# Rounding and splitting outputs at the head of a step, and the queries' rotary sums two slots later, in a prompt attention spread over 76 steps

## The reference, cut to what matters

```
q_nope, q_pe = q[..., :QK_NOPE], q[..., QK_NOPE:]
return q_lat, rope(q_pe, pos), rmsnorm(ckv, kv_norm), rope(kpe, pos)
...
s = jnp.where(kpos[None, :] <= qpos_b[:, None], s, -jnp.inf)
p = jax.nn.softmax(s, axis=-1).astype(ckv.dtype)
return jnp.einsum('bqhk,bkc->bqhc', p, ckv)
```

## Time and profile before

| | us |
|---|---|
| median of three runs | 1499.21 (1498.85 to 1500.34) |
| span of the profiled execution | 1494.5 |
| the profiled execution's own time | not listed; the median is 4.71 above its span |
| prompt attention in it, first scores to last split | 82.0 to 252.3 |
| an odd pair with eight pieces (three of them) | 24.9 |
| an even pair with four pieces (pairs 2, 4, 6) | 18.3 |
| pair 7 with its tail | 24.3 |

### The profile page before, as it was taken

How to read it: one execution, slowest core, us unless ns; L and a number is a source line. 1 busy time by engine, 2 the same in 40 slices (tenths; PEclk the granted TensorE clock), 3 DMA queues, 4 the chain that set the end, 5 groups by cost and what they waited for, 6 DMA issues and landing times.

```text
span 1494.5 us, 28951 instructions
## 1 busy us (share of the span) xinstructions
PE 1416.7 (95%) x11605; PEld 1292.3 (86%) x11605; DVE 695.9 (47%) x1128; ACT 493.1 (33%) x954; POOL 307.1 (21%) x268
## 2 busy tenths in 40 slices
PE   8988988799999999999998999999999999999997
PEld 7655655679899999999997788789989999999996
DVE  4456766524733433434446554535474343343434
ACT  5345544233521222212235334424352121221222
POOL 2210004201240511503410000000133051240530
PEclk9999998999999999999999999999999999999999
DMA  8400004222232222332222233223223223322221
GB/s 242 117 7 1 1 1 117 77 86 61 57 96 85 84 88 82 88 91 83 89 65 80 89 113 103 79 73 91 70 63 101 84 85 91 91 86 84 85 71 61
DMA packets 203905, 120.27 MB, mean 80 GB/s; under 512 B 13990, under 2 KB 199616, under 8 KB 203808
## 3 DMA queue, kind: packets, MB, share of 16 engines
q1 hardware_dynamic: 197776, 104.74, 24.4%
q0 software_dynamic: 6032, 14.17, 2.9%
HBM read 111.30 MB, written 7.59 MB: 80 GB/s over the span
## 4 chain that ended last, share of the span: by engine, by line
PE 85%; DVE 7%; ACT 3%; issue 2%; DMA 1%; POOL 0%; SPq 0%; DVEq 0%; ACTq 0%; POOLq 0%
PE ps L1867 61%; PE ps L1930 7%; PE ps L2087 2%; PE ps L2123 1%; DVE stat L1476 1%; PE ps L2181 1%; PE ps L2246 1%; ACT w_hi L821 1%; DVE y L1323 1%; PE ps L1891 1%; DVE x L1330 1%; PE ps L2264 1%; PE ps L2106 1%; DVE w_lo L1295 1%; DVE qT L1468 1%
## 5 line engine op out<-in xcount | busy, mean ns | idle before, releaser
L821 ACT CAST w_hi<-w_raw 128x1024 fp32r<-128x1024 f32 x172 | 180.2, 1049 | 680.7 <-PE ps L1867 653.7
L1867 PE MATMUL ps<-act_hi,w_hi 128*128 128x280 f32 (+1 forms) x1408 | 298.2, 293 | 7.7 <-DVE relu L1615 3.9
L1867 PE MATMUL ps<-act_hi,w_lo 128*128 128x280 f32 (+1 forms) x1408 | 296.0, 291 | 0.0
L1867 PE MATMUL ps<-act_lo,w_hi 128*128 128x280 f32 (+1 forms) x1408 | 294.9, 291 | 0.0
L1295 DVE TENSOR_TENSOR w_lo<-w_raw,w_hi 128x1024 fp32r<-128x1024 f32 x172 | 255.0, 1485 | 74.1 <-ACT w_hi L821 74.0
L1867 PEld LDWEIGHTS ps<-act_hi,w_hi 128*128 128x128 f32 x1408 | 223.9, 189 | 14.2 <-issue 13.0
L1867 PEld LDWEIGHTS ps<-act_hi,w_lo 128*128 128x128 f32 x1408 | 224.6, 190 | 0.0
L1867 PEld LDWEIGHTS ps<-act_lo,w_hi 128*128 128x128 f32 x1408 | 223.7, 190 | 0.0
L1867 PE MATMUL ps<-h_hi,w_lo 128*128 128x280 f32 (+1 forms) x928 | 193.6, 290 | 0.0
L1867 PE MATMUL ps<-h_hi,w_hi 128*128 128x280 f32 (+1 forms) x928 | 192.9, 289 | 0.0
L1867 PE MATMUL ps<-h_lo,w_hi 128*128 128x280 f32 (+1 forms) x928 | 192.8, 289 | 0.0
(11 more groups left out here) (327 smaller groups left out, 1899.0 us busy)
## 6 DMA issues: line engine op xcount, KB each, us to landing
w_raw<-in_mlp_w_up_dram SPq DMA_DIRECT2D x64, 512.0 KB, 4.1
w_raw<-in_mlp_w_down_dram SPq DMA_DIRECT2D x64, 512.0 KB, 3.8
w_raw<-in_gla_w_in_dram SPq DMA_DIRECT2D x24, 512.0 KB, 3.8
pg_ckv<-in_cache_ckv_dram SPq DMA_DIRECT2D x64, 128.0 KB, 2.3
w_raw<-in_mla_w_o_dram SPq DMA_DIRECT2D x8, 512.0 KB, 4.3
sts<-in_state_gla_dram POOLq DMA_DIRECT2D x4, 1024.0 KB, 6.3
out_dram<-sts POOLq DMA_DIRECT2D x4, 1024.0 KB, 5.1
w_raw<-in_gla_w_o_dram SPq DMA_DIRECT2D x8, 512.0 KB, 3.8
```

What stands on the lines that cost most here:

```text
L821: nc.scalar.copy(w_hi[slot(g)][:], w_raw[raw_slot(g)][:]).then_inc(w_rounded, 1)
L1867: last = nc.tensor.matmul(out[:, h, 0:n], w[:, c, :], a[:, c, t0 + n * h:t0 + n * h + n], start=(c == 0 and k == 0), stop=(c == DC - 1 and ...
```

## The change

On ACT, `round_out` goes ahead of the same step's `exp_scores`. On DVE, `split_out` goes ahead of the same step's `max_scores`. The rotary sums leave `take_piece` of QN1 and become `add_rotary(p, hh)`, one call for each head of the pair; `rotary_at` puts them behind the steps of the key pieces: k = 6 and 7 when the next pair is even, k = 4 and 6 when it is odd. Sums of pair 0 stay behind its pieces, ahead of the loop. No instruction is added or dropped; `add_rotary` repeats waits that `take_piece` had.

```
+def rotary_at(n):
+
+    p, k = n // UNITS, n % UNITS
+    at = (6, 7) if p % 2 else (4, 6)
+    return (p + 1, at.index(k)) if p + 1 < PAIRS and k in at else None
...
             for n in range(N_UNIT + 4):
+                if n >= 4 and out_at(n - 4) is not None:
+                    round_out(out_at(n - 4))
                 if n < N_UNIT:
                     exp_scores(n)
-                if n >= 4 and out_at(n - 4) is not None:
-                    round_out(out_at(n - 4))
...
                 last.then_inc(dve_piece, 1)
-                if a:
-                    dve.wait_ge(turned_queries, p // 2 + 1)
-                    dve.wait_ge(dve_piece, DVE_PIECE[p - p % 2, "RT1"] + 1)
-                    if p % 2 == 0:
-                        nc.vector.tensor_tensor(qrs[:, p // 2, :] ... ALU.add).then_inc(q_sampled, 1)
-                    for hh in range(2):
-                        k = ROPE * (2 * (p % 2) + hh)
-                        nc.vector.tensor_tensor(qT[2 * (p % 2) + hh][NOPE:QH, :], rope_q[k:k + ROPE, :], rope_tmp[k:k + ROPE, :],
-                                                ALU.add).then_inc(q_roped, 1)
+
+            def add_rotary(p, hh):
+                dve.wait_ge(turned_queries, p // 2 + 1)
+                dve.wait_ge(dve_piece, DVE_PIECE[p - p % 2, "RT1"] + 1)
+                if p >= 2:
+                    dve.wait_ge(s_mm, UNITS * (p - 1))
+                if p % 2 == 0 and hh == 0:
+                    nc.vector.tensor_tensor(qrs[:, p // 2, :] ... ALU.add).then_inc(q_sampled, 1)
+                k = ROPE * (2 * (p % 2) + hh)
+                nc.vector.tensor_tensor(qT[2 * (p % 2) + hh][NOPE:QH, :], rope_q[k:k + ROPE, :], rope_tmp[k:k + ROPE, :],
+                                        ALU.add).then_inc(q_roped, 1)
...
+            for hh in range(2):
+                add_rotary(0, hh)
             for n in range(N_UNIT + 4):
+                if n >= 4 and out_at(n - 4) is not None:
+                    split_out(out_at(n - 4))
                 if n < N_UNIT:
                     max_scores(n)
                 if 1 <= n < N_UNIT + 1:
                     norm_probs(n - 1)
-                if n >= 4 and out_at(n - 4) is not None:
-                    split_out(out_at(n - 4))
                 if n < N_UNIT and piece_at(n) in DVE_PIECE:
                     take_piece(*piece_at(n))
+                if n < N_UNIT and rotary_at(n) is not None:
+                    add_rotary(*rotary_at(n))
```

More of the change, by code:

```diff
@@ L1458, in take_piece @@
                 last.then_inc(dve_piece, 1)
-                if a:
-                    dve.wait_ge(turned_queries, p // 2 + 1)
-                    dve.wait_ge(dve_piece, DVE_PIECE[p - p % 2, "RT1"] + 1)
-                    if p % 2 == 0:
-                        nc.vector.tensor_tensor(qrs[:, p // 2, :].rearrange("p (s b) -> p b s", b=NB),
-                                                rope_q[:, NP:T].rearrange("p (b s) -> p b s", b=NB),
-                                                rope_tmp[:, NP:T].rearrange("p (b s) -> p b s", b=NB), ALU.add).then_inc(q_sampled, 1)
-                    for hh in range(2):
-                        k = ROPE * (2 * (p % 2) + hh)
-                        nc.vector.tensor_tensor(qT[2 * (p % 2) + hh][NOPE:QH, :], rope_q[k:k + ROPE, :], rope_tmp[k:k + ROPE, :],
-                                                ALU.add).then_inc(q_roped, 1)
+            def add_rotary(p, hh):
[4 more added lines that the diff above has]
+                if p % 2 == 0 and hh == 0:
+                    nc.vector.tensor_tensor(qrs[:, p // 2, :].rearrange("p (s b) -> p b s", b=NB),
+                                            rope_q[:, NP:T].rearrange("p (b s) -> p b s", b=NB),
+                                            rope_tmp[:, NP:T].rearrange("p (b s) -> p b s", b=NB), ALU.add).then_inc(q_sampled, 1)
+                k = ROPE * (2 * (p % 2) + hh)
+                nc.vector.tensor_tensor(qT[2 * (p % 2) + hh][NOPE:QH, :], rope_q[k:k + ROPE, :], rope_tmp[k:k + ROPE, :],
+                                        ALU.add).then_inc(q_roped, 1)
             def max_scores(n):
```

## The result

The changed kernel takes 1481.47 us (median; 1480.23 to 1482.72) against 1499.03 of the kernel before (1496.01 to 1500.34): ratio 0.9877, 95% interval 0.9859 to 0.9894, which is 15.9 to 21.1 us faster. The forecast was 14.7 us.

A forecast was written before the change was run, and what follows sets the result against it. PE was taken as the bound, waiting on DVE's and ACT's order, not their load. Odd pairs 9.3, even pairs 2.4, pair 0 1.1 and pair 7 1.9 sum to 14.7 us: 1499.21 to 1484.5, range 1480.8 to 1491.0.

The forecast's parts named there:

- the 0.70: Odd pairs: PE's 0.70 us wait stays, since ACT reads QR0 behind `place_probs`, which is not moved.
- 1.05, 0.40 and 0.61: Odd pairs: PE's waits at unit 8's output (bank 6), QN0 and KN0 close with rounding and splitting first.
- 1.02: Odd pairs: PE's 1.02 us wait at KN1 closes whole once the sums no longer delay unit 6's maximum.
- the 0.58: Even pairs: PE's single listed stop, for bank 6 at unit 8's output, closes with rounding and splitting first.
- forecast 1.1: Pair 0: the 1.42 wait at unit 2's transposition goes, 0.3 to 0.6 is lost at unit 6's; net 1.1 us.
- The late maxima: Maxima wait behind split and rounding, about 0.5 us late at a pair's change; costed at nothing where pieces cover it.
- rival B: Late maxima exposed at steps 0, 5, 7 of even pairs and pair 7 cost 5.3 us: 1489.8; chance 0.17.
- my 1.9: Pair 7 with its tail: 1.9 us gained, ends 1.0 and 2.3, as DVE's idle waits for rounding go.
- Rival C: Only the sums matter; PE's waits 1.05, 0.58 and 1.57 stay: 8.2 us gained, 1491.0; chance 0.04.
- D: DVE, five output steps of a pair: loop from output to transposition becomes the bound, net 9 us slower, 1508.5; chance 0.03.
- E: No change: stalls move to ACT's reading of the pieces and stay the same in sum, 1499; chance 0.02.
- The 3.4 us: Behind the stage, at latent queries: full clock could take up to 3.4 us off, or 3 be lost; taken as none.

The follow-up runs named there:

- e6_seven_only: Changed kernel, but rounding and splitting go first only for unit 7's output, the other four outputs keeping the old order: 1486.32 us, ratio 0.9915 to before.
- e3_sums: Kernel before with only the rotary sums moved to the key pieces' slots, rounding and splitting in the old order: 1491.41 us, ratio 0.9959 to before.
- e5_rotary_read_first: Changed kernel, with ACT reading QR0 and QR1 ahead of that step's copy of transposed probabilities: 1479.71 us, ratio 0.9881 to before.
- e2_order: Kernel before with only rounding and splitting put first, rotary sums left behind QN1: 1488.51 us, ratio 0.9940 to before.
- e7_five_late: Changed kernel, with the old order (maximum and exponential first) in steps n mod 9 = 0, unit 5's output: 1480.14 us, ratio 0.9883 to before.
- e8_best: Changed kernel, ACT reading QR0 and QR1 ahead of the probabilities' copy, old order in steps n mod 9 = 0 and 7: 1478.38 us, ratio 0.9876 to before.
- both comparisons: The changed kernel unmodified, timed twice against the kernel before: 1481.47 us, ratio 0.9877, and again on one chip 1480.67 us, ratio 0.9884.
- The control: The kernel before, unmodified, timed against itself: 1498.51 us, ratio 0.9994, single runs from 1495.82 to 1504.13 us.

## Why the prediction was right in its mechanism and short in its size

**The waits.** All four waits that were said to close in an odd pair closed, the 0.70 stayed, and each is carried by the edit named for it: 1.05, 0.40 and 0.61 by the order (e6_seven_only separates the first from the other two), 1.02 by the sums (e3_sums).

**The terms, which were too small.** "The granted clock is 1.00 in the pairs, so PE's work there stays as long as it is" is the step that failed, and with it the sum of bare idle times, 1.05 + 0.40 + 0.61 + 1.02 = 3.08. The odd pair gave 3.42. PE's busy time in it fell as well, from 21.15 to 20.81, since products that follow without a stop overlap in the rows. The gain isn't the same for every wait: the 1.02 at KN1 alone was worth 1.23 (e3_sums) and the 0.70 at QR1 0.91 (e5_rotary_read_first), 0.21 more each, while the other three, 2.06 together, were worth 2.19 (e2_order). The three odd pairs gave 10.2 for 9.3. The even pair gave 0.96 and not 0.8: 0.66 of idle time (the 0.58, and most of two stops under 0.1 that I left out when I wrote that it stops once) and 0.30 of busy time (17.58 to 17.28); three of them 2.9 for 2.4. Pair 0 gave 1.13 (forecast 1.1). Pair 7 gave 1.4 in length or, with the clock full in the tail, 2.6, and at one clock 2.1 (forecast 1.9). Together the stage gave 15.6 or 16.8, at one clock about 16.3, for 14.7.

**The attribution in even pairs was wrong.** I booked the 0.58 to the order alone. e2_order gives -0.05 there and e3_sums 0.30: the wait closes, but 1.50 of sums stand right behind it, and the late maximum at unit 7 costs 0.50. Only both together give 0.96.

**The late maxima.** Their place and size were right (about 0.5 at a pair's change). With the sums moved they cost nothing from pair 1 to 6 (e7_five_late, e8_best), so rival B falls there; in pair 0 they cost 0.4 to 0.5 (e8_best, e6_seven_only), as worked out, and in pair 7 the one at the pair's change 0.5 (e7_five_late), for the 0.3 to 0.4 inside my 1.9. Rival C falls by the row at 103.64, D and E by the result. As for the rule of strict FIFO queues in the Trainium skill ("PSUM — Partial Sum Buffer", Engine vs sequencer instructions): the trace agrees, the maximum at 119.35 stood behind a split that waited 0.76; it did no harm, as PE had other work in hand.

**Behind the stage, and the low end of the range.** Nothing changed there: 1242.0 us of span before, 1242.2 after. The 3.4 us by which the clock there might have changed the time, one way or the other, didn't come. In all profiles of this study it is 1239.9 to 1244.9, and the stretch ahead of the stage 80.3 to 84.2. The 4.71 between span and median that I carried over was mostly scatter: before's profiled execution took 1496.01 itself, 1.5 above its span. I gave the clock 3 us on the fast side and nothing to the terms there, though I took the closed waits of the odd pairs at their bare idle time, and they turned out worth that or more. So the end of the range, 1480.8, was set by a term that gave nothing, and the terms that gave more had no room: the ratio puts the time at 1499.21 x 0.9877 = 1480.77, just outside, and the median alone, 1481.47, just inside. That it comes so near the end is chance. What stays open is the 1 to 2 us by which the medians of both comparisons exceed the stage's gain in the profiles; both intervals (15.9 to 21.1 and 14.7 to 20.2 us) hold about 16.3 as well. The control has the size of such scatter in single runs but not in its ratio, and no run here tells whether another rhythm ahead shifts the low-clock stretches behind.

## What to carry to other kernels

When an engine's order puts the release of a buffer behind work that itself waits for the buffer's user, put the release first and ask what the newly waiting instruction holds up; here 0.5 us of lateness cost nothing under 1.2 us of other work, and about 0.5 where nothing covered it (pairs 0 and 7). Size a closed wait a little above its idle time, and look at what stands directly behind it on the helping engine: in even pairs one edit alone gave nothing because the other obstacle was next. Judge parts of 1 to 3 us by the length of the stage in the profile, which repeated to 0.02 us a pair, and not by medians of runs that scatter by 10. And before calling a gain absent, look at the durations of like products in both profiles: in e7_five_late a gain of 0.5 was hidden by one product at the lower clock.

## What the runs showed of the hardware that I had not expected

A wait of 0.70 us on PE that closed shortened the pair by 0.91 (e5_rotary_read_first), one of 1.02 by 1.23 (e3_sums), and four waits of 3.08 in all by 3.42. The granted clock fell to its lower level at different places in executions of nearly the same code: in the tail of pair 7 or only behind it (1.15 us of difference in that pair), in one profile inside pair 5 (1.3 us) and again in the middle of pair 7 (1.1 us), and ahead of the stage for more or less time (PEclk 0.96 to 1.00 over the first 80 to 84 us). Inside pair 5 the engine's last stop before the fall was 1.05 us long.
